# The last two quarters of the residual sum moved from VectorE to GpSimd

## The reference, cut to what matters

```
y = rms_norm(block(rms_norm(x, g_pre)), g_post)
x = x + 0.5 * y     # feed-forward
x = x + y           # attention
```

## Time and profile before

| what | value |
|---|---|
| time, median of 3 runs | 3156.38 us (3156.29 to 3156.52) |
| time of the profiled execution | 3159.18 us |
| its span | 3156.7 us |
| TensorE matmul busy | 2896.1 us, 92% |
| VectorE busy | 1600.9 us, 51% |
| ScalarE busy | 1097.2 us, 35% |
| GpSimd busy | 293.7 us, 9% |
| mean granted TensorE clock | 0.954 of full |
| L793, scaling a quarter of y | x48, 740 to 751 ns |
| L804, adding a quarter to x | x48, 679 to 693 ns |

### The profile page before, as it was taken

The page is one execution under the profiler, slowest core; times in us unless marked ns, Lnnn a source line. Parts: engine busy times, 40 slices in busy tenths (PEclk is TensorE's granted clock), DMA queues, the critical chain, the costliest instruction groups (busy, mean ns, idle before and its releaser), DMA issues.

```text
span 3156.7 us, 46606 instructions
## 1 busy us (share of the span) xinstructions
PE 2896.1 (92%) x17949; PEld 2478.6 (79%) x17949; DVE 1600.9 (51%) x2328; ACT 1097.2 (35%) x1592; POOL 293.7 (9%) x458
## 2 busy tenths in 40 slices
PE   7987999998879999988999998799895689999999
PEld 6985698997747989975798997499653458999998
DVE  4643456653254566523455653466206635655565
ACT  4334334432163344313334442443103114333433
POOL 0011000101020010001000100110201000000000
PEclk9999999999889999999999999899997789999999
DMA  8432454453404545433454543354331034545542
GB/s 290 181 113 94 167 181 178 173 186 105 160 1 168 198 160 199 160 113 120 167 194 165 181 179 106 114 187 179 90 137 48 27 121 160 186 173 199 179 180 93
DMA packets 329017, 474.31 MB, mean 150 GB/s; under 512 B 8952, under 2 KB 266320, under 8 KB 328944
## 3 DMA queue, kind: packets, MB, share of 16 engines
q1 hardware_dynamic: 325120, 462.93, 41.1%
q0 software_dynamic: 3408, 10.26, 1.2%
q10 hardware_dynamic: 416, 0.15, 0.0%
HBM read 472.21 MB, written 1.10 MB: 150 GB/s over the span
## 4 chain that ended last, share of the span: by engine, by line
PE 87%; DVE 8%; ACT 2%; POOL 2%; issue 1%; DMA 0%; ACTq 0%; DVEq 0%; PEldq 0%; POOLq 0%
PE psum_all L1173 15%; PE psum_all L1175 15%; PE psum_all L1174 15%; PE psum_all L1210 7%; PE psum_all L1211 7%; PE psum_all L1212 7%; PE psum_all L1262 6%; PE psum_all L1273 5%; PE psum_all L1577 4%; DVE attn_max L1467 1%; PE psum_all L1838 1%; PE psum_all L1387 1%; PE psum_all L1408 1%; DVE x_scaled L793 1%; PE psum_all L1368 1%
## 5 line engine op out<-in xcount | busy, mean ns | idle before, releaser
L1173 PE MATMUL psum_all<-hT_hi,gu_hi 128*128 128x256 f32 x3840 | 1097.1, 286 | 23.0 <-DVE gu_lo L1016 10.5
L1174 PE MATMUL psum_all<-hT_lo,gu_hi 128*128 128x256 f32 x3840 | 1094.9, 285 | 0.0
L1175 PE MATMUL psum_all<-hT_hi,gu_lo 128*128 128x256 f32 x3840 | 1094.7, 285 | 0.0
L1173 PEld LDWEIGHTS psum_all<-hT_hi,gu_hi 128*128 128x128 f32 x3840 | 745.0, 194 | 37.1 <-DVE gu_lo L1016 11.1
L1174 PEld LDWEIGHTS psum_all<-hT_lo,gu_hi 128*128 128x128 f32 x3840 | 745.1, 194 | 8.7
L1175 PEld LDWEIGHTS psum_all<-hT_hi,gu_lo 128*128 128x128 f32 x3840 | 744.8, 194 | 0.0
L1016 DVE TENSOR_TENSOR gu_lo<-raw_ring,gu_hi 128x2048 fp32r<-128x2048 f32 x240 | 549.7, 2292 | 65.4 <-ACT gu_hi L1004 64.1
L1038 ACT ACTIVATE silu_gate<-silu_gate 128x256 f32<-128x256 f32 x240 | 100.3, 418 | 1112.8 <-DVE silu_gate L1092 1112.7
L1004 ACT ACTIVATE gu_hi<-raw_ring 128x2048 fp32r (+1 forms) x240 | 456.0, 1902 | 7.2 <-DVE oT L1493 6.9
L1210 PE MATMUL psum_all<-down_hi,hidden_hi 128*128 128x512 f32 x960 | 378.0, 394 | 4.6 <-DVE hidden_lo L1100 4.1
L1211 PE MATMUL psum_all<-down_lo,hidden_hi 128*128 128x512 f32 x960 | 376.8, 393 | 0.0
(11 more groups left out here) (294 smaller groups left out, 2126.8 us busy)
## 6 DMA issues: line engine op xcount, KB each, us to landing
raw_ring<-in_ffn_w_in SPq DMA_DIRECT2D x176, 1024.0 KB, 7.0
raw_ring<-in_w SPq DMA_DIRECT2D x96, 1024.0 KB, 7.5
raw_ring<-in_ffn_w_out SPq DMA_DIRECT2D x88, 1024.0 KB, 9.1
raw_ring<-in_c_w_in SPq DMA_DIRECT2D x12, 768.0 KB, 5.3
gain<-in_norm_g POOLq DMA_DIRECT2D x16, 512.0 KB, 4.4
raw_ring<-in_w_in SPq DMA_DIRECT2D x10, 768.0 KB, 5.4
raw_ring<-in_a_w_in SPq DMA_DIRECT2D x8, 768.0 KB, 5.1
raw_ring<-in_b_w_in SPq DMA_DIRECT2D x8, 768.0 KB, 5.2
```

The lines of the kernel that those rows point to most:

```text
L1173: nc.tensor.matmul(out, w_hi, K.hT_hi[:, k, :], start=k == 0, stop=False)
L1174: nc.tensor.matmul(out, w_hi, K.hT_lo[:, k, :], start=False, stop=False)
L1175: return nc.tensor.matmul(out, w_lo, K.hT_hi[:, k, :], start=False, stop=k == KT - 1)
```

## The change

In the twelve passages, the adds of the third and the fourth quarter (`x_order(after)[2:]`) are taken off VectorE and put at the end of `pool_post` on GpSimd, as a TENSOR_TENSOR add after a wait for `y_scaled`. The two other adds stay on VectorE, as a TENSOR_TENSOR too. The factor 0.5 goes into the root: with four times the mean and four times epsilon, the root comes out halved, so that `x_scaled` is already half. VectorE's four scalings stay.

```diff
@@ pool_post
+    after = K.blocks[b["n"] + 1]
     for a in range(NT):
         ...
-        K.plink(pool, nc.gpsimd.tensor_scalar(v, v, 1.0 / D, EPS, ALU.mult, ALU.add))
+        four = 4.0 if b["kind"] == "ffn" else 1.0
+        K.plink(pool, nc.gpsimd.tensor_scalar(v, v, four / D, four * EPS, ALU.mult, ALU.add))
         nc.gpsimd.tensor_tensor(st[:, POST_R + a:POST_R + a + 1], v, K.minus_half, ALU.pow).then_inc(K.sem.r_post, 1)
+    for h, a in x_order(after)[2:]:
+        x = K.x[:, a, half(h)]
+        pool.wait_ge(K.sem.y_scaled, 4 * b["p"] + x_order(after).index((h, a)) + 1)
+        nc.gpsimd.tensor_tensor(x, K.xs[:, a, half(h)], x, ALU.add).then_inc(K.sem.x_new, 1)
@@ dve_add_y
     if has_post(b):
-        after = K.blocks[b["n"] + 1]
-        dve.wait_ge(K.sem.y_scaled, 4 * b["p"] + x_order(after).index((h, a)) + 1)
-        K.nc.vector.scalar_tensor_tensor(out=x, in0=K.xs[:, a, half(h)], scalar=0.5 if b["kind"] == "ffn" else 1.0,
-                                         in1=x, op0=ALU.mult, op1=ALU.add).then_inc(K.sem.x_new, 1)
+        turn = x_order(K.blocks[b["n"] + 1]).index((h, a))
+        if turn >= 2:
+            return
+        dve.wait_ge(K.sem.y_scaled, 4 * b["p"] + turn + 1)
+        K.nc.vector.tensor_tensor(x, K.xs[:, a, half(h)], x, ALU.add).then_inc(K.sem.x_new, 1)
```

## The result

The changed kernel takes 3168.53 us (median of 6 runs, 3165.61 to 3171.53). The kernel before took 3156.25 us in its runs beside it (6 runs, 3150.62 to 3156.52). The ratio is 1.0041, with a 95% interval of 1.0028 to 1.0054: slower by 0.41%, some 12 to 13 us. The forecast was 3163.8 us in a range of 3157.0 to 3169.5. The direction and the mechanism were right; the size was 7.4 us where 12.3 were measured.

The account below looks back on a forecast made before the run. TensorE bounds the kernel, losing time only where it stands still, as in passages between blocks. GpSimd's queue 5.45 us plus clock 2.0 us make 7.4 us on 3156.38: 3163.8 us, range 3157.0 to 3169.5.

Parts of the forecast that it names:

- step 2: Passage into a mixer: tile 0's chain stands behind both GpSimd adds, its root ready at 224.17 in place of 222.63.
- Nothing is gained on tile 1: Passage into a mixer: GpSimd's second add ends at 223.08, where the last quarter was there at 223.07 before.
- the feed-forward passages are covered: Seven passages into a feed-forward: 2.0 to 2.4 us of cover before TensorE needs the last quarter, so no cost.
- The queue's term: Five passages into a mixer: second transposes 1.09 us later in each, 5.45 us in all.
- the clock's: TensorE's granted clock in the five mixer passages: +2.4 us, rounded down to +2.0 us as a guess.
- the forecast's own case: Both terms, GpSimd's queue and TensorE's clock, are paid: 5.5 to 11 us slower, chance 0.57.
- step 3: Passage into a mixer: VectorE's first norm waits for tile 0's root; first transposes start 1.22 us later.
- step 4: Passage into a mixer: tile 1's chain follows, held up by the norm; second transposes begin 1.09 us later.
- my own signs: Profile of changed kernel: GpSimd adds 1.0 to 1.15 us, first norm 1.2 us later, TensorE idle 8.6 to 8.9 us.
- the clock gives some or all of it back: Mixer passages: queue paid, clock 0 to -4 us, chance 0.24; or clock saves 6.5 against 5.45 us, chance 0.08.
- the one that the add is far off: GpSimd's add far from 1.04 us: 3172.4 us at 1.90, 3159.5 us at 0.61; chance 0.08, three quarters upwards.
- The one that the change does nothing: Mixer passages: tile 0's chain is not really behind the adds; 3156.4 us, chance 0.03.

Follow-up runs that it names:

- e5: Kernel before, all its adds on VectorE, plus two unused adds on GpSimd in each of the five passages into a mixer; 3166.6 us, ratio 1.0039.
- e2: Changed kernel, but adds moved to GpSimd only in the seven passages into a feed-forward; 3153.5 us, ratio to before 0.9999.
- e1: Changed kernel with all 24 moved adds back on VectorE, only the factor in the root kept; 3155.7 us, ratio to before 1.0003.
- e3: Changed kernel, but adds moved to GpSimd only in the five passages into a mixer; 3170.1 us, ratio to before 1.0047.
- e4: Changed kernel with tile 0's root made ahead of the two GpSimd adds in the mixer passages; 3175.5 us, ratio to before 1.0062.
- e9: Kernel before with unused identity matmuls filling TensorE's idle stretches ahead of mixers (32) and feed-forwards (9, 3, 12); 3132.8 us, ratio 0.9919.
- e12: Changed kernel with 40 unused identity matmuls ahead of a mixer's transposes alone; 3154.4 us, ratio to before 0.9988.
- e6: Kernel before with 50 unused identity matmuls, too many, ahead of a mixer's transposes; 3160.0 us, ratio 1.0016.

## Why the prediction was right in its mechanism, and short in size

**Place and mechanism: right.** The chain named in step 2 (tile 0's root behind both adds in GpSimd's queue) is what the profile after shows, and e5 shows it alone. "Nothing is gained on tile 1" held too. That the feed-forward passages are covered was shown by e2, that root and plain add are free by e1, and that it is all in the mixer passages by e3.

**The miss** is 12.3 - 7.4 = 4.9 us. The queue's term is 1.7 of it, the clock's, which had to hold all else, the other 3 or so. It also takes the result beyond the 5.5 to 11 us of the forecast's own case; the upper end of the range, 3169.5, was 1 us away.

**The first term that was mis-sized: GpSimd's add.** I took 1.04 us from the multiply by a broadcast coefficient, the row of the same width. It was 1.267. The figure that the Trainium skill gives ("GPSIMD Engine Reference", section 3.1) makes an estimate of 1.12 us, which was the nearer one and still low. Through the steps: the adds end 0.45 us later than in my sum, and the first transposes start 226.55 - 0.52 - 224.32 = 1.71 us later where step 3 had 1.22. The second eight of the sixteen start at 228.55, which is 228.55 - 0.52 - 226.59 = 1.44 us later where step 4 had 1.09. A part of the error is taken back in between: tile 1's root was ready 0.69 us after the end of the first norm, and step 4 had 0.81. Five passages: 7.15 us in place of 5.45. Two of my own signs failed by this term: the adds were to take 1.0 to 1.15 us, and TensorE's idle stretch was to be 8.6 to 8.9 us (it was 9.24 to 9.27).

**The second term: the clock, near at the mixers, not priced elsewhere.** I had put +2.0 us on the five passages: the two early rises missed, the first passage won, the two late ones shortened. This profile has each of these. The third and fourth first projections lost 1.8 and 2.0 us (I had 2.2 each) and their second transposes 0.35 and 0.31; the first projections won 1.6, and the second and fifth 0.4 and 0.75. The five mixers' 8.5 us less 7.15 for the queue are 1.4 us. What I did not price is that everything behind starts later too: a balance of 2.4 us more. The sum of the profile is 7.15 + 1.37 + 2.42 + 0.06 = 11.0 us.

That one execution fits the guess so well is luck. In e3's, with the same queue ahead of mixers, all five first projections ran slow, the first in 16.57 us. The profiled executions together say that it is no fair coin. With the adds of before ahead of mixers, three, one and one of five first projections ran slow (before, e1, e2); with adds on GpSimd there, four, five, five and three did (changed kernel, e3, e4, e5). So the change seems to make the loss of clock more frequent, which seven executions suggest and don't prove. It also bears on the 1.3 us by which the medians lie further apart than the profiles: the profile of before is that of a slow execution, 3159.2 us with three slow projections, and those of e1 and e2 took 3150.0 and 3153.2 with one each.

**The bound for a measurement.** The first three runs of before agreed within 0.23 us, but later runs of the same kernel lie over 11 us, from 3149.7 to 3160.9. My bound of 6.3 us was wide enough: the interval of the change's ratio is some 4 us to either side, and 12.3 us are clear of it. The granted clock goes with a run's time: 0.958 of full in the run of 3149.7 us, 0.953 in that of 3160.9. That fits a clock term that falls out anew in each execution. The runs of e9 to e12 spread by 3 to 7 us, but they are 5 to 11 runs each against 23 and 28, so that less spread is not shown by them.

**The rivals.** Those that the clock gives some or all of it back did not come, it took more; the one that the add is far off came in part, a fifth above my value, not near the upper bound. The one that the change does nothing is refuted by e3.

## What to carry to other kernels

Before work is moved to an idle engine, look at what stands behind it in that engine's queue at that place. GpSimd was 9% busy, but its tiny chain for tile 0 was on the path, and VectorE's spare 1.4 us bought nothing, since the longer adds delayed tile 1's end as well. Take the price of an instruction from a row with the same kinds of operands, not only the same width. And where TensorE idles between blocks for several us, a shift of about one us can win or lose clock (1.6 us won at the first passage here, 2.2 lost at the third): compare kernels over many runs, or hold the clock up in both before you judge.

## What the runs showed of the hardware that I had not expected

- GpSimd's add of two full float32 tensors, 128x512, took 1.267 us, and the multiply by a broadcast coefficient of the same width 1.035 us.
- Work that nobody uses made the kernel faster: e9 makes 244 more products of 128x128, which are 976 instructions, matmuls and weight loads together (47582 against 46606), and is 0.8% faster than the kernel before.
- A single float32 matmul of 128 columns cost 0.228 us (11.40 us for 50 in e6), a transpose of the same size 0.14 us (1.09 us for eight), both at the higher clock.
- A tiny GpSimd instruction on 128x1, L741, took 1.19 us in place of 0.19 beside VectorE's norm of x, and ended with it.
- Eight transposes took 1.97 us at the lower clock and 1.09 at the higher. The clock rose in the midst of a row of transposes in the third passage before the change (1.62 us for the second eight).
